# Gates at slots for the last two experts of a routed-expert stage, and an earlier read-back of the other rows

## The reference

```python
h = h + hier_moe(rmsnorm(h, ffn_norm[layer]), ...)       # end of layer 0 and of layer 1
# hier_moe: the best of 4 groups, in it the best 2 of 8 experts, for each row
gate = p_grp * softmax(top_v)                            # two gates a row
y_e = (silu(x @ w_gate[e]) * (x @ w_up[e])) @ w_down[e]  # 32 experts, 1024 x 512 weights
y = sum over the row's two experts of gate * y_e
kv = rmsnorm(h, kv_norm) @ w_kv                          # behind layer 0
out = rmsnorm(h, final_norm)                             # behind layer 1
```

## Time and profile before

| | us |
|---|---|
| median of 3 runs | 1586.99 |
| lowest, highest | 1578.34, 1589.73 |
| span of the profiled execution | 1583.6 |
| PE busy | 1356.3 |
| DVE busy | 402.2 |
| ACT busy | 314.8 |
| POOL busy | 190.8 |

### The profile page before, as it was taken

How to read it: one execution, slowest core, us unless ns; L and a number is a source line. 1 busy time by engine, 2 the same in 40 slices (tenths; PEclk the granted TensorE clock), 3 DMA queues, 4 the chain that set the end, 5 groups by cost and what they waited for, 6 DMA issues and landing times. The chain is left out here.

```text
span 1583.6 us, 17830 instructions
## 1 busy us (share of the span) xinstructions
PE 1356.3 (86%) x6818; PEld 760.2 (48%) x6818; DVE 402.2 (25%) x751; ACT 314.8 (20%) x605; POOL 190.8 (12%) x309
## 2 busy tenths in 40 slices
PE   5999997998878887887999878897998988878886
PEld 4999774333323232323789656783333322323232
DVE  3344424000000000004535688524000000000003
ACT  5212221111000000002433266330111000000002
POOL 2000001111111111111000000001111111111111
PEclk9999997999999999999999989997999999999999
DMA  9130447999999999997313200456999999999995
GB/s 341 57 108 1 160 163 299 402 425 425 424 427 425 425 425 425 426 425 286 125 59 118 86 34 1 160 195 255 414 425 424 425 427 426 425 426 423 425 424 203
DMA packets 63099, 473.75 MB, mean 299 GB/s; under 512 B 11232, under 2 KB 11308, under 8 KB 38976
## 3 DMA queue, kind: packets, MB, share of 16 engines
q1 hardware_dynamic: 48656, 442.55, 68.0%
q0 software_dynamic: 14384, 30.36, 5.2%
HBM read 465.17 MB, written 23.13 MB: 308 GB/s over the span
## 5 line engine op out<-in xcount | busy, mean ns | idle before, releaser
L1105 PE MATMUL ps<-ring,act 128*64 128x512 f32 x1792 | 443.2, 648 | 77.4 <-DMA ring<-in_e_up 63.7
L1105 PEld LDWEIGHTS ps<-ring,act 128*64 128x64 f32 x1792 | 140.8, 142 | 374.7 <-issue 374.7
L1654 DVE TENSOR_TENSOR act<-act,ps 128x256 f32<-128x256 f32 x64 | 27.0, 422 | 867.7 <-ACT act L889 867.7
L1128 PE MATMUL ps<-ring,act 128*64 128x512 f32 x896 | 204.6, 597 | 31.0 <-ACT act L891 31.0
L1070 PE MATMUL ps<-parts 128*128 128x512 f32 x576 | 141.1, 403 | 8.6 <-DVE parts L1457 7.7
L1043 PE MATMUL ps<-parts 128*128 128x264 f32 x1152 | 144.0, 287 | 4.5 <-DVE parts L1449 2.9
L1043 PEld LDWEIGHTS ps<-parts 128*128 128x128 f32 x1152 | 142.7, 190 | 5.5 <-issue 5.5
L889 ACT ACTIVATE act<-ps 128x256 f32<-128x256 f32 x64 | 24.6, 384 | 551.5 <-PE ps L1105 551.5
L1128 PEld LDWEIGHTS ps<-ring,act 128*64 128x64 f32 x896 | 70.8, 136 | 126.2 <-issue 126.2
L1070 PEld LDWEIGHTS ps<-parts 128*128 128x128 f32 x576 | 109.5, 193 | 36.8 <-issue 6.4
L1330 PE MATMUL ps<-parts 128*128 128x264 f32 (+1 forms) x576 | 92.4, 322 | 1.2 <-PE ps L1330 0.9
(11 more groups left out here) (212 smaller groups left out, 1055.6 us busy)
## 6 DMA issues: line engine op xcount, KB each, us to landing
ring<-in_e_gate SPq DMA_DIRECT2D x56, 2048.0 KB, 18.0
ring<-in_e_up SPq DMA_DIRECT2D x56, 2048.0 KB, 22.5
ring<-in_e_down SPq DMA_DIRECT2D x56, 2048.0 KB, 22.3
arena<-in_e_down SPq DMA_DIRECT2D x8, 2048.0 KB, 16.1
ring<-in_a_w_in SPq DMA_DIRECT2D x6, 2048.0 KB, 20.6
arena<-in_e_up SPq DMA_DIRECT2D x6, 2048.0 KB, 19.8
arena<-in_e_gate SPq DMA_DIRECT2D x6, 2048.0 KB, 14.8
ring<-in_w_kv SPq DMA_DIRECT2D x4, 2048.0 KB, 13.4
```

The source lines that it names most:

```text
L1105: last = mm(ps[f * C:(f + 1) * C, 2 + b, :].rearrange("p (g m i) -> p g m i", g=2, i=2), x, w, start=(k == 0), stop=(k == KC - 1))
L1128: last = mm(ps[o * C:(o + 1) * C, 6 + b, :], hT[:, b, (2 * c + a) * C:(2 * c + a + 1) * C], w[:, f * D + o * DH:f * D + (o + 1) * DH], sta ...
```

## The change

Expert 30 is treated as expert 31 was. Both results stay on the chip (`last_y[0]`, `last_y[1]`), each with its own matrix of gates at slots, and neither is scattered. At the start two zero scatters stand where one stood. DVE makes the second matrix behind the first `xT` (`mark_gates(0)`), PE turns it inside the first expert (`turn_gates(0, 7, 5)`), and DVE copies it out (`place_gates`). The read-back is issued behind the scatter of expert 29. `combine` of tiles 0 to 2 stands, on DVE, between the `hidden` of expert 30 and the `hidden` of expert 31; tile 3, and in layer 0 tile 4, follow behind the `hidden` of expert 31. In both layers a tile takes two passes now, and the diagonal products of layer 1 are gone. PE adds expert 30's rows (`add_rows(.., 0)`) ahead of expert 31's.

```diff
@@ pool (the queue of scatters and read-backs)
-                pool.indirect_dma_start(y_halves[layer], bass.IndirectOffsetOnAxis(dst_row[:, E - 1:E], 0), zero, None,
-                                        bounds_check=4 * SPREAD - 1, oob_is_err=False).then_inc(zeroed, 16)
+                for e in (E - 2, E - 1):
+                    pool.indirect_dma_start(y_halves[layer], bass.IndirectOffsetOnAxis(dst_row[:, e:e + 1], 0), zero, None,
+                                            bounds_check=4 * SPREAD - 1, oob_is_err=False).then_inc(zeroed, 16)
...
-                pair(PAIRS - 1, False, True)
-                pool.wait_ge(zeroed, 16 * (layer + 1))
+                pool.wait_ge(zeroed, 32 * (layer + 1))
                 for b in range(2):
-                    pool.wait_ge(scattered[layer][b], 16 * (PAIRS - b))
+                    pool.wait_ge(scattered[layer][b], 16 * (PAIRS - 1))
@@ scalar
+                    if first and u == 0:
+                        act.wait_ge(last_marked, 2 * layer + 2)
...
-                    nc.scalar.copy(last_y if final else y_out[:, u, :], ps[:, 6 + u, :]).then_inc(y_ready, 1)
+                    nc.scalar.copy(last_y[u] if final else y_out[:, u, :], ps[:, 6 + u, :]).then_inc(y_ready, 1)
@@ tensor
+                    if last_pair and u == 1:
+                        add_rows(layer, 0, 0)
+                    else:
...
+                    if first and u == 0:
+                        turn_gates(0, 7, 5)
...
+            def add_rows(layer, t, e):
+
+                pe.wait_ge(y_ready, E * (layer + 1) - 1 + e)
                 for a in range(2):
-                    last = mm(last_rows(layer, t)[:, a, :], last_gate(t)[a * C:(a + 1) * C, :], last_y[a * C:(a + 1) * C, :], start=not both, stop=True)
-                last.then_inc(last_done, 1)
+                    rows_of = slice(a * C, (a + 1) * C)
+                    last = mm(last_rows(layer, t)[:, a, :], last_gate(layer, e, t)[rows_of, :], last_y[e][rows_of, :], start=(e == 0), stop=(e == 1))
+                if e == 1:
+                    last.then_inc(last_done, 1)
 
             moe(0)
+            for t in (1, 2):
+                add_rows(0, t, 0)
...
             moe(1)
+            for t in (1, 2):
+                add_rows(1, t, 0)
             for t in range(NX):
-                add_last(1, t)
+                if t == NX - 1:
+                    pe.wait_ge(y_ready, 2 * E)
+                    add_rows(1, t, 0)
+                add_rows(1, t, 1)
@@ vector
+                dve.wait_ge(last_marked, 2 * layer + 1)
+                mark_gates(0)
+                dve.wait_ge(zeroed, 32 * (layer + 1))
+                one(0, 0, False)
+                place_gates()
+                one(0, 1, False)
...
                 one(PAIRS - 1, 0, True)
+                for t in range(NX - 1):
+                    combine(layer, t)
                 one(PAIRS - 1, 1, True)
+                for t in range(NX - 1, nt):
+                    combine(layer, t)
...
-                order(v.scalar_tensor_tensor(h[0:r, t, :], y_in(t, 0), gate[0:r, 0, t:t + 1], h[0:r, t, :], ALU.mult, ALU.add))
-                if not by_product(layer, t):
-                    order(v.scalar_tensor_tensor(h[0:r, t, :], y_in(t, 1), gate[0:r, 1, t:t + 1], h[0:r, t, :], ALU.mult, ALU.add))
+                for k in range(2):
+                    order(v.scalar_tensor_tensor(h[0:r, t, :], y_in(t, k), gate[0:r, k, t:t + 1], h[0:r, t, :], ALU.mult, ALU.add))
@@ vector, behind moe(0)
+            take_last(0, 0)
             weight_low(S_KVQ)
-            combine(0, 0)
-            take_last(0, 0)
-            weight_low(S_KVQ + 1)
-            combine(0, 1)
+            take_last(0, 1)
             act_low(T_KVQ)
-            take_last(0, 1)
-            weight_low(S_KVQ + 2)
-            weight_low(S_KVQ + 3)
+            for i in range(1, QUARTERS):
+                weight_low(S_KVQ + i)
+            take_last(0, 2)
             act_low(T_KVQ + 1)
...
```

More of the change, by code:

```diff
@@ L713, in pair @@
                         nc.gpsimd.tensor_copy(dst_now[:, u:u + 1], dst_row[:, bass.ds(q * 2 + u, 1)]).then_inc(index_set[layer], 1)
[L714 removed]
+                        pool.wait_ge(index_set[layer], n + 2)
                         alone()
@@ L891, in one @@
                     nc.scalar.copy(hT[:, u, :], ps[:, 4 + u, 0:FE // 2]).then_inc(hT_ready, 1)
-                    if final and layer == 0:
-                        weight_high(S_KVQ)
-                        weight_high(S_KVQ + 1)
                     if lead:
@@ L920, in moe @@
                     pair(q, False)
-                one(PAIRS - 1, 0, False)
-                one(PAIRS - 1, 1, False, True)
+                for u in range(2):
+                    one(PAIRS - 1, u, False, True)
             moe(0)
-            weight_high(S_KVQ + 2)
-            weight_high(S_KVQ + 3)
+            for i in range(QUARTERS - 1):
+                weight_high(S_KVQ + i)
             act_high(T_KVQ)
+            weight_high(S_KVQ + QUARTERS - 1)
             act_high(T_KVQ + 1)
@@ L1192, in one @@
                     (gs, gv), (us, uv), (ds, dv) = (expert_unit(layer, q, u, part, early) for part in ORDER)
+                    if first and u == 1:
+                        pe.wait_ge(last_placed, layer + 1)
                     if lead:
@@ L1343, in _ @@
                     pe.wait_ge(act_low_ready, T_KVQ + p + 1)
-                    add_last(0, p + 2)
+                    for e in range(2):
+                        add_rows(0, p + 2, e)
                 project(p, p + 1 if 2 <= p + 1 <= NX else None)
@@ L1868, in finish @@
                 v.scalar_tensor_tensor(result[:, t, :], h[:, t, :], rstd[:, t:t + 1], final_gain, ALU.mult, ALU.mult).then_inc(final_ready, 1)
-            for t in range(NX - 1):
-                combine(1, t)
             for t in range(NX):
                 take_last(1, t)
-                if t == 0:
-                    combine(1, NX - 1)
-                else:
+                if t >= 1:
                     finish(t - 1)
```

106 lines of the change are left out of this document (51 added, 55 removed).

## The result

The changed kernel takes 1604.8 us, median of 4 runs (1602.77 to 1606.93). The kernel before took 1583.17 us on the same chip (4 runs, 1578.34 to 1589.73). The ratio is 1.0126, with a 95% interval of 1.0104 to 1.0147: the change makes the kernel slower, by about 20 us by the ratio (the two medians are 21.6 us apart).

What follows compares the result with a forecast made beforehand. Weight loads were taken to pace most of a stage, the read-back to bind layer 1's end and a DVE chain layer 0's. 5.0 + 9.3 + 1.0 = +15.3 us on 1586.99 gave about 1602, range 1588 to 1611.

Steps and rivals of the forecast that it cites:

- Steps 1 and 2: Read-back at both layers' ends: starts 13 to 14 us earlier, tile 2 lands at 1562.0 (layer 1) and 740.2 (layer 0).
- Step 3: DVE at layer ends: hidden of expert 31 waits behind tile 2's combine, +7.9 us in layer 1, +11.5 in layer 0.
- Step 4: From hidden of expert 31 to take_last: 5.25 us, plus 1.6 for PE's lower clock, plus 3.1 for adds.
- Step 5: End of layer 1: 14.05 us from take_last of tile 0 to the end, making layer 1's end +5.0 us.
- Step 6: End of layer 0: first projection ends 7.3 us later, two more adds of 1.0 follow, +9.3 us.
- Step 7: Start of both layers: five gate transposes cost 0.5 us a layer, +1.0 us in all, bounds zero to 2.
- balanced engines: Rival, 20%: DMA engines make up their lag, tile 2 lands at 1555.1 and 732.9; +1 us, 1588.
- read-back in time: Rival, 8%: tiles 0 to 2 are combined before silu of expert 31, delaying nothing; -5 us, 1582.
- case of a slow PE: Rival, 15%: POOL's loads end last and PE stays at the lower clock through down and adds; +24 us, 1611.
- (1): Sign at both layers' ends: POOL's first read-back load goes out at about 1541 and 716.
- (6): Sign at layer ends: DVE does not wait behind take_last of tile 0.
- (4): Sign in the DMA queues: q1 and q0 side by side, q0 near a fifth, expert 31's up weights 1 to 2 us later.

Runs made afterwards that it cites:

- e5: Changed kernel with early combines moved behind hidden of expert 31, some expert 30 adds later, silu's table loaded early; layers 0 and 1 take 516.8 and 490.7 us.
- e6: e5 with the read-back also waiting for expert 30's rows, issued 6 and 4.5 us later; layers 0 and 1 take 517.1 and 489.5 us.
- e1: Changed kernel with combines of tiles 0 to 2 moved behind hidden of expert 31; gives back 2.7 of 11.5 us in layer 0, 4.5 of 6.7 in layer 1.
- e8: Kernel before with only combines of tiles 0 to 2 moved ahead of hidden of expert 31; costs 11.4 us in layer 0 and 11.8 in layer 1.
- e2: Changed kernel with a one-column silu ahead of ACT's new wait, loading silu's table early; layers 0 and 1 take 523.4 and 498.3 us.
- e4: Changed kernel with PE's pause before hidden of expert 31 filled by constant products; down takes 3.65 us, layers 0 and 1 regain 4.0 and 1.2 us.
- e7: e5 with the read-back issued from SyncE's queue behind the weights; layers 0 and 1 take 514.5 and 490.2 us.
- e3: Changed kernel reading back only the first choice of tiles 0 to 3; hidden of expert 31 comes 5.4 and 3.5 us earlier in layers 0 and 1.

## Why the prediction was right, and where it was not

**Steps 1 and 2, issue and landing.** Right. The read-back starts 8.7 and 9.0 us behind the scatter of 29 (8.6 and 8.8 forecast). By the forecast tile 2 lands 29.3 us behind that scatter in layer 1 and 32.4 in layer 0. In layer 0 its combine starts at 31.97, having waited. In layer 1 the last wait is tile 1's, and combine 2 follows without one, but the landing of tile 2's second load, the sixth of the eight, issued at about 1559.7, is on record:

```profile
arena<-expert_rows POOLq DMA_DIRECT2D x1, 512.0 KB, 18.0
```

It landed at 1577.7, 29.7 behind the scatter, against 29.3. The rate of 425 GB/s, for which the prediction names no row, is near what its rows 4 give (2.58 MB in 6 us, 430). That a few engines lag is the prediction's reading of a share and a landing; no view here tells the engines apart, so the time is confirmed and the lag is not.

The share of POOL's queue was wrong: I carried the 21% of the earlier trace rows over, and it was 46.0 and 40.9%. In 1559:1565 the mean packet is 9.4 KB on q1 and 3.8 KB on q0, with two packets of q0 to one of q1, not packet by packet in turn. The sum didn't hang on the share, because it was built on when all bytes have been moved. The key and value weights took 8.9 us longer from issue to landing than before, which I had not priced. It cost nothing in the changed kernel, where they landed ahead of their first use (ACT's split at 755.26, landing at 748.8), but ACT waits for them once the order is repaired (e5, e6). The Trainium skill (Trainium Kernel Development and Optimization, section Key Constraints) says that DMAs issued from the SP, ACT and POOL queues run on the same 16 DMA engines and interleave. The trace agrees: in 1559:1565 the two queues have 53.1 and 46.0% of these engines, 99.1% together.

**Step 3, `hidden` behind the combines.** Right: +8.6 in layer 1 and +11.1 in layer 0, forecast +7.9 and +11.5. e1 and e8 show that the place of the combines does it, and e8 that it does it alone.

**Step 4, from `hidden` to take_last.** 10.5 and 11.1 us, forecast 9.95. The slow clock costs 2.2 and 2.75 us in down, not 1.6. The row I sized it by had a pause of 2.7 us, and here the pauses were 7.7 and 10.3; that a longer pause costs more isn't shown, since in e2 a down of 5.10 follows a pause of 9.57 and one of 6.09 a pause of 8.06. e4 shows the mechanism.

**Step 5, the end of layer 1.** +5.0 forecast, +6.2 measured from the scatter; from take_last to the end 14.0 us, forecast 14.05.

**Step 6, the end of layer 0.** +9.3 forecast, +10.3 measured (8.1 and 2.2). I gave 7.3 us to the late `hidden` and 2.0 to two adds; up to the end of the first projection it was 8.1, behind it 2.2, of which the rows give the adds 1.7 (each 0.9 more than the single add before). Both terms were about right for this kernel, though PE's pauses among the projections before, which the step puts at 0.3 us or less, read up to 0.36. The two terms aren't what repairing the order would give back: the order alone costs 11.4 (e8, whose read-back is later as well), and with the order repaired (e5 to e7) layer 0 still stands 2.5 to 5.1 us above before. The two come to more than the 11.5 of the whole, so they overlap. Once `hidden` is early, PE waits behind the first projection and its adds run in part at the lower clock, which the late `hidden` had covered.

**Step 7, the starts.** 0.5 us each forecast. Locally it was 3.1 and 1.4 us (16.0 and 14.3 against 12.9). The step missed the price of ACT's new wait, the 1.28 us of table load; the other 1.7 in layer 0 are the down product of 5.35 us, which e3 and e4 don't have with the same start. By the scatter of 29, 1.3 and 0.5 are left, within that scatter's own wandering, and e2 shows that mending it changes neither layer.

**The sum.** 15.3 forecast. The same steps measured are 6.2 + 10.3 + 1.8 = 18.3; the other 3.2 of the 21.5 lie where nothing changed. The forecast time was 1602, the median 1604.8. That the two times lie so near is in part luck: the change was forecast at 15.3 us and measured at about 20, but the forecast started from 1586.99, the median of three runs of the kernel before, and the median of four was 1583.17. Of the chances, 0.55 stood on a change within 1% and 0.43 on a loss of over 1%; the loss was 1.26%, so the less likely of the two came.

**The rivals.** The balanced engines needed tile 2 at 22.4 us behind the scatter of 29 in layer 1, and even tile 0 came at 23.95. The read-back in time needed tile 2 before silu, and it was missed by over 5 us (tile 2 there at 743.9 and 1577.7, silu at 735.8 and 1572.4). The case of a slow PE was half there: PE was at the lower clock for the first 4 us of down in layer 1 and over 5 in layer 0, then was granted full speed, also in the adds. Of the signs listed, (1), (2), (3) and (5) are in the rows above; (6) held but for 0.41 us ahead of the first `rstd` of layer 1; of (4), the up weights landed 0.8 us later and q0's share was twice what I said.

## What to carry to other kernels

Before moving work ahead of an instruction on its engine, ask what that instruction releases: DVE's combine is not urgent, the `hidden` behind it is what PE waits for, and putting six passes that hang on a late transfer in front of it cost more than all else in the change. Don't take the landing of a transfer from its issue when the queues are full: here an issue 4.5 to 6 us earlier moved tiles 0 to 2 by less than 2 us, some of them later, and 2 MB of weights beside the read-back took 9 to 11 us longer to land. And a local loss among the first experts can be gone at the last ones, so cut the span at both places before pricing it.

## What the runs showed of the hardware

- A read-back issued 4.5 to 6 us earlier into loaded queues landed its first tile 0.3 us later to 1.1 us earlier, and its third 1.0 later to 1.2 earlier (e6 against the changed kernel).
- A load of 2 MB beside it took 27.2 to 29.1 us from issue to landing where it took 18.3 before (changed kernel, e5, e6).
- Two queues do not split by fixed turns: q0 had 21.0% beside 81.1% for a store of 512 KB, and 46.0% beside 53.1% for eight loads of 512 KB.
- After PE pauses of 7.73 and 10.31 us, a product of 3.65 us took 5.81 and 6.40; with the pause filled, 3.65. After 9.57 us it took 5.10 (e2).
- A second wait ahead of the first silu moved the table load of 1.28 us from 256.75 to 275.56, between gate_up and the silu.
